# Encoder layer step: second feed-forward product by frame, first product in half tiles over three banks

## The reference, cut to what matters

```python
x = x + rmsnorm(merged @ w_out, g_post_mix)
hf = rmsnorm(x, g_pre_ffn)
hf = jnp.square(jax.nn.relu(hf @ w_ff1)) @ w_ff2      # 1024 -> 4096 -> 1024
x = x + rmsnorm(hf, g_post_ffn)                       # eps 1e-6
```

## Time and profile before

| | |
|---|---|
| median of 3 runs | 1274.06 us (1274.03 to 1274.21) |
| profiled execution | 1272.26 us |
| its span | 1270.3 us |
| mean granted TensorE clock | 0.993 |
| busy: PE, PEld, DVE, ACT, POOL | 97%, 94%, 57%, 31%, 2% |
| instructions | 21064, of which 8354 matmuls |
| HBM read, written | 100.36 MB, 14.21 MB |

### The profile page before, as it was taken

How to read it: one execution, slowest core, us unless ns; L and a number is a source line. 1 busy time by engine, 2 the same in 40 slices (tenths; PEclk the granted TensorE clock), 3 DMA queues, 4 the chain that set the end, 5 groups by cost and what they waited for, 6 DMA issues and landing times.

```text
span 1270.3 us, 21064 instructions
## 1 busy us (share of the span) xinstructions
PE 1234.8 (97%) x8354; PEld 1194.7 (94%) x8354; DVE 730.0 (57%) x1274; ACT 396.2 (31%) x579; POOL 20.2 (2%) x33
## 2 busy tenths in 40 slices
PE   7999999999999999999999999899999999999995
PEld 7998999999899988899998988899999999999995
DVE  5634579879896989788364546343243334333434
ACT  5442343233223323212156232232132123114332
POOL 2000000000000002000000000000000000000000
PEclk9999999999999999999999999999999999999998
DMA  8343442262226332323222262122222222222212
GB/s 238 99 120 96 116 118 70 84 170 75 83 84 164 78 101 75 84 67 100 68 68 65 83 227 56 34 71 80 83 67 84 67 73 75 83 67 71 79 34 83
DMA packets 186286, 115.61 MB, mean 91 GB/s; under 512 B 13791, under 2 KB 180919, under 8 KB 186210
## 3 DMA queue, kind: packets, MB, share of 16 engines
q1 hardware_dynamic: 165026, 94.58, 26.8%
q10 hardware_dynamic: 21184, 20.02, 5.0%
HBM read 100.36 MB, written 14.21 MB: 90 GB/s over the span
## 4 chain that ended last, share of the span: by engine, by line
PE 52%; issue 39%; DVE 4%; ACT 3%; DMA 1%; SPq 0%; DVEq 0%; ACTq 0%; POOLq 0%; POOL 0%
PE out L374 39%; PE bank L1480 5%; PE bank L1475 3%; PE out L1742 3%; PE bank L1742 2%; DVE WK L956 2%; DVE CV L956 1%; DMA WK<-in_x_prompt 1%; DVE WL L303 1%; PE out L355 1%; ACT CV L566 1%; ACT GH L566 0%; ACT WH L295 0%; ACT L566 0%; DVE WK L953 0%
## 5 line engine op out<-in xcount | busy, mean ns | idle before, releaser
L374 PE MATMUL out<-XH,WH 128*128 128x328 f32 (+1 forms) x1504 | 349.4, 313 | 2.2 <-DVE WL L303 2.2
L374 PE MATMUL out<-XH,WL 128*128 128x328 f32 (+1 forms) x1504 | 347.5, 312 | 0.0
L374 PE MATMUL out<-XL,WH 128*128 128x328 f32 (+1 forms) x1504 | 346.6, 311 | 0.0
L374 PEld LDWEIGHTS out<-XH,WH 128*128 128x128 f32 x1504 | 251.6, 188 | 6.8 <-issue 5.0
L374 PEld LDWEIGHTS out<-XH,WL 128*128 128x128 f32 x1504 | 252.3, 188 | 3.3 <-issue 3.1
L374 PEld LDWEIGHTS out<-XL,WH 128*128 128x128 f32 x1504 | 252.5, 188 | 2.9 <-issue 2.7
L303 DVE TENSOR_TENSOR WL<-ST,WH 128x1024 fp32r<-128x1024 f32 x149 | 182.5, 1225 | 123.6 <-ACT WH L295 106.1
L295 ACT ACTIVATE WH<-ST 128x1024 fp32r<-128x1024 f32 x147 | 154.8, 1053 | 233.7 <-PE out L374 183.2
L956 DVE SCALAR_TENSOR_TENSOR CV<-WK,cwu,CV 128x512 f32 (+1 forms) x480 | 226.4, 541 | 0.0
L374 PE MATMUL out<-GH,WH 128*128 128x320 f32 x768 | 176.6, 311 | 6.0 <-DVE WL L303 4.6
L374 PE MATMUL out<-GL,WH 128*128 128x320 f32 x768 | 175.6, 310 | 0.0
(11 more groups left out here) (189 smaller groups left out, 772.4 us busy)
## 6 DMA issues: line engine op xcount, KB each, us to landing
ST<-in_w_in SPq DMA_DIRECT2D x65, 512.0 KB, 4.1
ST<-in_w_ff SPq DMA_DIRECT2D x64, 512.0 KB, 4.1
WK<-in_state_mlstm_C ACTq DMA_DIRECT2D x32, 256.0 KB, 4.1
o_C_sample<-WK ACTq DMA_DIRECT2D x32, 256.0 KB, 2.5
WK<-in_x_prompt SPq DMA_DIRECT2D x8, 512.0 KB, 7.3
ST<-in_w_branch_m SPq DMA_DIRECT2D x8, 512.0 KB, 5.0
ST<-in_w_branch_c SPq DMA_DIRECT2D x8, 512.0 KB, 4.1
ST<-in_w_out SPq DMA_DIRECT2D x8, 512.0 KB, 3.6
```

Of the source, the lines that this page charges most:

```text
L374: last = pe.matmul(out[s][:, h, 0:H], w[:, s, kk, :], x[:, kk, h * H:(h + 1) * H], start=(m < 2), stop=(m >= len(ms) - 2))
```

## The change

The tiles of w_ff2 are loaded as two k blocks x 512 outputs (`load_rows`). In the second product 128 frames are the stationary side (GH, GL) and 512 outputs the moving side (WH, WL), over five banks, for output half 0 and then half 1; a chunk's result is added to `yt`, which lies by frame in the place of CV. In the last chunk the four tiles of half 1 go to XH2 and XL2, which the first product has left, so that the five frame groups finish one after the other; each is squared by ACT, scaled by its gain (loaded once into gpf), normalised and stored by itself. The transposes, the frame sums and the adding up of squares are removed.

The first product goes in half tiles (`units`): 24 matmuls into one bank, the banks used in turn out of three (F_BANK), a relu of 320 columns after each half. In chunk 0 the order of the first four halves is (tile 0, half 0), (1, 0), (0, 1), (1, 1). On ACT the weight copy of a tile stands ahead of the relu of the first half; at the start of chunk 0 it stands ahead of the relu of tile 0's second half. Three new counts (fu, t_f, ya) take the place of the counts of0 and of1 here.

In the cut diff the lines taken out are left away; they stand in the kernel above.

```diff
+    gpf, ysq = wk(z0, D), wk(z0 + 6 * T, 512)
+    yt = CV[:, :, :].rearrange("p k t -> p (k t)").rearrange("p (c e) -> p c e", c=5)
...
+    def load_rows(sp, n, w, k0, col):
+        need = sp.snap(val(n) - (NSTAGE - 1))
+        k0 = sp.snap(k0)
+        sp.wait_ge(sem(f"ld{n.par}"), 16)
+        sp.wait_ge(sem("w_lo"), need)
+        sp.dma_start(w_rows(ST, n.par), w[:, bass.ds(k0, 2), col:col + 512]).then_inc(sem(f"ld{n.par}"), 16)
+    def resident(n):
+        return isinstance(n.i, int) and n.i == LASTC and n.base >= N_FF0 + KT + 4
     def split_hi(act, n, par):
...
+        if n.per == 2 * KT and resident(n):
+            src, ks = out_split(par, n.base - N_FF0 - KT - 4)
+            wait(act, "tile_done", N_FF0 + 2 * KT * LASTC + KT)
+            act.activation(XH2[:, ks, 0:512], src, ACT.Copy).then_inc(sem("w_hi"), 1)
...
+            dve.tensor_tensor(XL2[:, ks, 0:512], src, XH2[:, ks, 0:512].bitcast(F32), ALU.subtract).then_inc(sem("w_lo"), 1)
...
+    F_BANK = (out[1][:, 0, :], out[0][:, 0, :], out[1][:, 1, :])
+    Y_BANK = ((B4, B5, B6, B7, out[0][:, 1, :]), F_BANK + (B4, B5))
+    LASTC = DFF // D - 1
+    def units(c):
+        us = [(r, h) for r in range(KT) for h in range(2)]
+        if isinstance(c, int) and c == 0:
+            us[0:4] = [(0, 0), (1, 0), (0, 1), (1, 1)]
+        return us
...
+                    load_rows(sp, n + (KT + r), w_2, c * KT + 2 * (r % 4), (r // 4) * 512)
+            sp.wait_ge(sem("zg"), 10)
+            dma(gpf, a["g_post_ffn"].to_broadcast([P, D]), "gpf")
...
+            def y_square(h, x):
+                act.wait_ge(sem("ya"), 10 * LASTC + 5 * h + x + 1)
+                wait(act, "ysq", 5 * h + x)
+                act.activation(ysq, yt[:, x, 512 * h:512 * h + 512], ACT.Square,
+                               accum_out=colH[:, 5 * h + x:5 * h + x + 1]).then_inc(sem("ysq"), 1)
             def ffn(c, last=False):
                 n = N(N_FF0, 2 * KT, c)
+                early = isinstance(c, int) and c == 0
+                for u, (r, h) in enumerate(units(c)):
+                    if early and r < 2:
+                        if u == 2:
+                            hi(n + 2)
+                    elif h == 0:
                         hi(n + (r + 1))
+                    if h == 0:
+                        act.wait_ge(sem("t_f"), c * KT + (r + 1))
+                    else:
+                        act.wait_ge(sem("tile_done"), val(n + r) + 1)
+                    copy(tmp[4 + r % 2][:, h * HALF2:(h + 1) * HALF2], F_BANK[u % 3][:, 0:HALF2], "fu", ACT.Relu)
+                    if h == 0:
+                        continue
                     act.wait_ge(sem("hsq"), c * KT + (r + 1))
                     copy(GH[:, r, :], tmp[2 + r % 2], "hh")
                     if last and r < 5:
                         act.wait_ge(sem("x2g"), 5)
                         wait(act, "fsq", r)
+                        act.activation(x2sq, x_of(r), ACT.Square, accum_out=sm[:, 30 + r:31 + r]).then_inc(sem("fsq"), 1)
+                for r in range(KT if not last else KT - 1):
+                    hi(n + (KT + 1 + r))
+                if last:
+                    for h in range(2):
+                        for x in range(5):
+                            y_square(h, x)
...
+            def y_add(c, h, x, n):
+                if x < 4:
+                    dve.wait_ge(sem("t_y"), 8 * c + (4 * h + x + 1))
+                else:
+                    dve.wait_ge(sem("tile_done"), val(n + (KT + 4 * h + 3)) + 1)
+                o = yt[:, x, 512 * h:512 * h + 512]
+                if isinstance(c, int) and c == 0:
+                    dve.tensor_copy(o, Y_BANK[h][x]).then_inc(sem("ya"), 1)
+                else:
+                    tt(o, Y_BANK[h][x], o, ALU.add).then_inc(sem("ya"), 1)
+            def y_gain(h, x):
+                dve.wait_ge(sem("ysq"), 5 * h + x + 1)
+                o = yt[:, x, 512 * h:512 * h + 512]
+                tt(o, o, gpf[:, 512 * h:512 * h + 512], ALU.mult).then_inc(sem("yg"), 1)
             def ffn(c, last=False):
                 n = N(N_FF0, 2 * KT, c)
+                early = isinstance(c, int) and c == 0
                 for r in range(KT):
+                    if not early or r:
                         lo(n + (r + 1))
+                    dve.wait_ge(sem("fu"), 3 if early and r == 0 else c * (2 * KT) + (2 * r + 2))
                     tt(tmp[2 + r % 2], tmp[4 + r % 2], tmp[4 + r % 2], ALU.mult).then_inc(sem("hsq"), 1)
                     dve.wait_ge(sem("hh"), c * KT + (r + 1))
                     tt(GL[:, r, :], tmp[2 + r % 2], GH[:, r, :].bitcast(F32), ALU.subtract).then_inc(sem("hl"), 1)
+                if not last:
+                    for h in range(2):
+                        for t in range(4):
+                            lo(n + (KT + 4 * h + t + 1))
+                        for x in range(5):
+                            y_add(c, h, x, n)
+                    return
+                for r in range(KT - 1):
+                    lo(n + (KT + 1 + r))
+                ffn_factors()
+                dve.wait_ge(sem("gpf"), 16)
+                for x in range(5):
+                    y_add(c, 0, x, n)
+                for x in range(5):
+                    y_gain(0, x)
+                for x in range(5):
+                    dve.wait_ge(sem("t_y"), 8 * LASTC + 4 + x + 1)
+                    o = yt[:, x, 512:D]
+                    tt(o, Y_BANK[1][x], o, ALU.add).then_inc(sem("ya"), 1)
+                    y_gain(1, x)
+                    V.link(stt(colH[:, 10 + x:11 + x], colH[:, x:x + 1], colH[:, 5 + x:6 + x], sm[:, 24 + x:25 + x],
+                               ALU.add, ALU.mult))
+                    dve.tensor_scalar(colH[:, 10 + x:11 + x], colH[:, 10 + x:11 + x], EPS, None, ALU.add
+                                      ).then_inc(sem("yvar"), 1)
+                    dve.wait_ge(sem("yrt"), x + 1)
+                    V.link(tt(colH[:, 20 + x:21 + x], colH[:, 15 + x:16 + x], sm[:, 18 + x:19 + x], ALU.mult))
+                    dve.wait_ge(sem("yg"), 5 + x + 1)
+                    stt(x_of(x), yt[:, x, :], colH[:, 20 + x:21 + x], x_of(x), ALU.mult, ALU.add).then_inc(sem("ytok"), 1)
...
+            def unit(c, n, r, h, u):
+                n, ins = n + r, None
+                s = n.par % 2
+                wait(pe, "w_lo", val(n) + 1)
+                if u >= 3:
+                    pe.wait_ge(sem("fu"), c * (2 * KT) + (u - 2))
+                elif not isinstance(c, int) or c:
+                    pe.wait_ge(sem("ya"), 10 * c - 4 + u)
                 for kk in range(KT):
                     for i, (w, x) in enumerate(((WH, XH2), (WH, XL2), (WL, XH2))):
+                        ins = pe.matmul(F_BANK[u % 3][:, 0:HALF2], w[:, s, kk, :], x[:, kk, h * HALF2:(h + 1) * HALF2],
                                         start=(kk == i == 0), stop=(kk == KT - 1 and i == 2))
+                ins.then_inc(sem("tile_done" if h else "t_f"), 1)
+            n = N(N_FF0, 2 * KT, 0)
             pe.wait_ge(sem("fl"), 3)
+            pe.wait_ge(sem("zg"), 9)
+            unit(0, n, 0, 0, 0)
+            unit(0, n, 1, 0, 1)
             x2_by_channel(4)
             pe.wait_ge(sem("fl"), 5)
             pe.wait_ge(sem("zg"), 10)
+            unit(0, n, 0, 1, 2)
+            unit(0, n, 1, 1, 3)
+            def y_part(c, h, x, kk, w_h, w_l, name=None):
+                cs = slice(x * P, x * P + P)
+                for i, (g, w) in enumerate(((GH, w_h), (GL, w_h), (GH, w_l))):
+                    ins = pe.matmul(Y_BANK[h][x], g[:, kk, cs], w, start=(kk == i == 0), stop=(kk == KT - 1 and i == 2))
+                if name:
+                    ins.then_inc(sem(name), 1)
             def ffn(c, last=False):
                 n = N(N_FF0, 2 * KT, c)
+                early = isinstance(c, int) and c == 0
+                for u, (r, h) in enumerate(units(c)):
+                    if not early or u > 3:
+                        unit(c, n, r, h, u)
+                for h in range(2):
+                    if last and h:
+                        break
+                    for t in range(4):
+                        m = n + (KT + 4 * h + t)
+                        pe.wait_ge(sem("w_lo"), val(m) + 1)
+                        w_h, w_l = w_rows(WH, m.par % 2), w_rows(WL, m.par % 2)
+                        for x in range(5):
+                            if t == 0 and h == 1:
+                                if x == 0:
+                                    pe.wait_ge(sem("fu"), c * (2 * KT) + 2 * KT)
+                                elif x > 2:
+                                    pe.wait_ge(sem("ya"), 10 * c + (x - 2))
+                            for k_ in range(2):
+                                if h == 0 and x == 0:
+                                    pe.wait_ge(sem("hl"), c * KT + (2 * t + k_ + 1))
+                                name = "tile_done" if x == 4 else "t_y" if t == 3 else None
```

(55 more changed lines are left out.)

59 lines of the change are left out of this document (4 added, 55 removed).

## The result

| | before | after |
|---|---|---|
| median of 4 runs each, on one chip | 1274.13 us (1274.03 to 1276.52) | 1257.72 us (1255.3 to 1258.48) |
| profiled execution, its span | 1272.26, 1270.3 us | 1255.3, 1253.6 us |
| first projection matmul to last matmul, start to start | 518.31 us | 509.45 us |
| last matmul's end to the end of the span | 15.42 us | 7.70 us |

The ratio is 0.9868, 95% interval 0.9855 to 0.988: 16.4 us faster, where 13.0 were forecast.

A forecast was written before the change was run, and what follows sets the result against it. TensorE's back-to-back matmuls and the serial tail were taken to bound the kernel; -2.9 + 0 + 0.7 - 3.3 + 0 - 7.5 = -13.0 us gave a forecast of 1261.0 us, range 1258.8 to 1264.2 us.

The forecast's parts named there:

- Step 1: Second product: 960 matmuls of 512 columns at 231.6 ns replace 1536 of 320 at 146.7 ns; -2.9 us (-3.5 to -2.3).
- Step 2: First product in half tiles: same 48 matmuls per tile at the same rate, added waits already met; 0 (0 to +1.3 us).
- Step 3: Start of chunk 0: weight copy ahead of a relu delays tile 2, so TensorE waits longer; +0.7 us (0 to 0.7).
- Rival A: Clock falls at the longer stall in chunk 0, 1.6 us lost, 1262.6 us in all; chance 12%.
- Step 4: Last chunk: transposes of the result go from six tile periods, 0.545 us each; -3.3 us.
- Step 5: Evacuation, weight copies and loads in the second product stay hidden behind matmuls, nothing waits; 0 us.
- Step 6: Tail: four of five last groups finish beside matmuls, 7.93 us remain against 15.44; -7.5 us (-8.1 to -6.6).
- B: Second product: a matmul's cost beside its columns is smaller, halving the gain of Step 1; 1262.5 us; chance 5%.
- C: Last half: DVE-ACT-POOL blocks exceed the 5.56 us period, last store 4.2 us later; 1265.2 us; chance 5%.
- D: Second product: TensorE's reads lose pace with weights moving, slower than before from 245.1 ns per matmul; chance 4%.

The follow-up runs named there:

- e2: Changed kernel with frames and resident weights in XH and XL in rows of 640 elements from byte 0, not 656 from byte 64; 1255.41 us, ratio 0.9859.
- e3: Changed kernel with the second product's stationary side in chunks 0 to 2 read from XH2 and XL2, not GH and GL (wrong output); 1261.37 us, ratio 0.9907.
- e10: Kernel before the change, with only its frames in XH and XL moved to rows of 640 elements from byte 0; 1273.09 us, ratio 0.9999.
- e9: Changed kernel with each 512-column second-product matmul in chunks 0 to 2 cut into two of 256 columns (wrong output); 1267.4 us, ratio 0.9948.
- e6: Changed kernel with the last chunk's second half run by weight tiles, all five frame groups ready only at its end; 1262.32 us, ratio 0.9911.
- e4: Changed kernel with chunk 0's tile 2 weight copy behind tile 0's relu on ACT, its low part ahead of GL on DVE; 1255.36 us, ratio 0.9865.
- e5: Changed kernel with 640-element rows, frames starting 64 bytes off, resident weight pairs 0, 64, 128 and 256 bytes off; 1257.47 us, ratio 0.9869.
- e8: Changed kernel with the edits of e2 and e4 together; 1255.7 us, ratio 0.986.

## Why the prediction was wrong, step by step

Direction and mechanism were right, and the price of one term was not; the time came out 3.3 us lower. In the stretches, 518.31 + 15.42 = 533.73 us became 517.15: -16.6 where the steps gave -13.0.

- **Step 1 failed, by its size.** It priced all 960 matmuls at the projection's 231.6 ns. The 840 in 28 weight tiles took 226.7 ns (28 x 6.80 = 190.4 us), the 120 of the resident half 231.7 ns (27.8 us): 218.2 us in place of 225.3, **-7.1 us and not -2.9**. This -4.2 us is more than the whole miss. The mechanism is the one predicted: 576 matmuls fewer at 13.3 ns each are 7.7 us, less 0.6 us for the 120 slow ones. The projection reads frames, and then frames are not at a multiple of 512 bytes; the second product reads GH and WH, which were not slowed. e2 took the penalty away, and e3 brought it into the second product, at close to the sizes expected. The stated lower bound, -3.5 us, came from the spread of three groups of the same kind, and so could not hold a price that belongs to the operand's place. The bound from the other form stood in the earlier trace rows: 146.7 ns less 320 / 2.4 leaves 13.3 ns, and 512 columns with the same 13.3 ns give 226.7. The rule of the Trainium skill weighed in the prediction ("TensorE: Matmul & The Clock Gate", section "Back-to-back issue gap") has this form with 2.5 ns and gives it for an isolated matmul; the form holds for the stream here, and the 2.5 ns does not: the traces have 13.3 ns.
- **Step 2** was forecast at 0, with bounds of 0 to +1.3 us for additional waits. It came to +0.8 us, inside the bounds but for another reason: a tile took 7.04 us, not 7.01, in most of the 32, and there was no wait for a relu. The halves in chunk 0 of before that the step took as its measurement had run at 146.0. It is the pace of 146.1 or 146.7 ns told under e10, which the order of the matmuls alone does not set.
- **Step 3** held: the wait is 1.6 us in place of 1.1, and the tile starts 0.5 us later (+0.6 against its stage). Rival A did not come. The granted clock behind it (second row) stayed at 1.00, 2.4 GHz; behind the 2.4 us of idle (first row, answering to the earlier trace rows) it was at 1.2 GHz again.

```profile
805.60:809.00 3.40, 3.35 (x13) 3.35 (x14) 0.00 (x0) 0.00 (x0) 0.00 (x0) 0.52 0.00 0
816.10:819.50 3.40, 3.37 (x23) 3.37 (x24) 2.47 (x3) 1.69 (x2) 0.00 (x0) 1.00 0.51 142
```

- **Step 4** held: no transposes in the last chunk, -3.3 us.
- **Step 5** held: no wait at a turn of a chunk or half. The 1.5 us of e9 came where the loop jumps back and not for a bank or weights.
- **Step 6** held: 7.70 us against 7.93 forecast, so -7.7 us; the chain took 4.67 us (4.73) and the store with the end 3.03 us (3.2). e6 shows that the resident half, and not the frame layout alone, earns it.
- Sum of the steps as measured: -7.1 + 0.8 + 0.6 - 3.3 - 7.7 = -16.7 us, 0.1 us from the stretches' -16.6. The projection, which was not changed, took 0.1 us more.
- **Range.** Its upper end does not follow from its bounds: they add up to -10.2 us, so to 1263.9 us and not 1264.2. Nothing hangs on it here. The lower end could not hold the result, because the bounds of step 1 ended at -3.5 us.
- **Rivals.** B is refuted: it halved the gain of step 1, and the gain was more than twice the forecast. C did not come: the stores stay 5.56 us apart. D did not come: no matmul form in the second product slowed.

```profile
1228.34 0.36 SPq L439 DMA_DIRECT2D o_y_sample<-WK  x1
1233.89 17.02 SPq L439 DMA_DIRECT2D o_y_prompt<-WK  x4
```

What stays open: what picks the pace of 146.1 or 146.7 ns for a chunk, why a start off 512 bytes costs at all, and what TensorE stood for at the jump back in e9.

## What to carry to other kernels

Take the price of a new matmul form from two sides: from the nearest row of that form, and from the other form's cost beside its columns; where they differ, look at where the operands lie, and widen the range to both. Then look at what is finished last: a final product arranged so that its groups end one after the other was worth 6.1 us of tail here, 5.4 us net of what its layout cost. And with TensorE at 97% busy, a stall is still worth its length and the slow clock behind it: moving eight transposes by one half tile gave 3.9 us.

## What the runs showed of the hardware

- A matmul of this kind costs its columns at 2.4 GHz and 13.3 ns more: 120.0, 146.7 and 226.7 ns at 256, 320 and 512 columns. The trace has one load of the stationary side per matmul, at 256 columns too, where two in a row use the same one.
- A 512-column matmul costs 5 to 7 ns more (231.6 to 233.3 in place of 226.7 ns) if its operand lies in rows that do not start at a multiple of 512 bytes from the tensor's start. Tried were 64, 128 and 256 off for the moving side, and 64 off and the rows of 656 elements for the stationary side. At 320 columns nothing of the kind was seen: 146.1 ns from the unaligned rows and 146.7 from the aligned ones, in the old kernel.
- The 320-column matmuls of the first product have two paces, 146.1 and 146.7 ns, and a chunk keeps to one of them; e3, e4 and e9 show both within one execution.
- In 12 profiled executions TensorE idled 2.4 us behind transposes; in 10 the granted clock then fell, in two (e5, e9) it did not. After the 1.6 us behind dense matmuls it fell in none of the eight executions that had this wait. What decides it was not settled.
- The projection began between 736.0 and 740.6 us in kernels that are the same up to there but for where the frames lie. The start follows the stretches at 1.2 GHz ahead of it, which lie between 30 and 694 us: with one of them 736.0 to 736.5 us, with two 737.1 to 738.3, with three 739.4 to 739.5 (e8, e9), and 740.6 in e5, with three of which one was twice as long. A change of 2 us in a later stage is seen in its stretch before it is seen in the median.
